# The low part of every fourth weight unit, moved from VectorE to a negating ScalarE pass and an adding DMA

## Chip, core and metric

One core of one Trainium2 chip. The metric is the time of one execution in microseconds on the device; lower is better. The profiler shows the TensorE matmul queue (PE), its weight loads (PEld), VectorE (DVE), ScalarE (ACT), GpSimd (POOL) and the DMA queues of SyncE (SPq) and of GpSimd (POOLq).

## What is computed

Two transformer-like layers follow one another on 256 tokens of width 2048, in float32. Each layer has a mixing part (projections, a state-space or delta-rule scan, an attention) and then the MLP, and only the MLPs are touched here:

```python
u = rmsnorm(x, g_mlp) @ w_up                    # first layer: 2048 -> 8192
x = x + jnp.square(jax.nn.relu(u)) @ w_down     # 8192 -> 2048
...
h = rms_norm(x, ln2_w)                          # second layer
x = x + jnp.square(jax.nn.relu(h @ w_up)) @ w_down
return rms_norm(x, ln_f_w)
```

## The kernel before

**Weights.** Every matmul operand is split in two: a high part in the rounded format `fp32r`, and a low part, the value less its high part. A product is three matmuls: high by high, high by low, low by high (L558 to L560 in the MLPs). Weights come from HBM in pieces of 128 x 2048 floats (1 MB) into `ring`, which has four places; SP issues these transfers in the order of use (L2972), each when the low parts of the piece four places earlier have been made. A piece is two units of 128 x 1024. For unit `u`, ScalarE copies the unit into `w_hi[:, u % 4]` (L2163), which rounds it, and VectorE subtracts that from the ring's value into `w_lo[:, u % 4]` (L1295). ScalarE may start when TensorE is done with unit `u - 4`; TensorE may start unit `u` when `unit_lo` says that its low part is there. There are four places for units, so a unit's place becomes free three units ahead of its first matmul.

**The MLPs.** The first runs over units 122 to 377, the second over units 628 to 883. Each does four rounds `f` of an up part and a down part, both 32 units. A part is four blocks `n` of 512 columns, a block eight units; a unit is 12 matmuls of 512 columns, back to back. Below, the place of a unit in its block is 0 to 7.

**What comes between.** When TensorE has made an up block, ScalarE applies relu and the square (`relu_squared`, L2472 and L2477) ahead of the copy of the next block's place 3; VectorE turns the block in two halves (`turn_up`, L1695), one after its low part of place 4 and one after that of place 5; ScalarE then makes the block's high part (`squared_hi`, L2483) ahead of the copy of place 7; and VectorE makes its low part (L1703). In the first down block of a round, which turns the fourth up block, the first half comes ahead of VectorE's low part of place 3, and `squared_hi` ahead of the copy of place 6. Each engine works through its list in this fixed order, which is written by hand:

```python
for i in range(8):                    # ScalarE, an up block
    if n > 0 and i == 0:
        relu_squared(b - 1)
    split_to(unit + UNITS)            # the copy of unit + 3
    unit += 1
    if n > 0 and i == 3:
        squared_hi(b - 1, hid)
```

**GpSimd.** It does nothing in the MLPs but fold squares for the norms at their ends (L2862) and issue a few transfers there.

Of the kernel before, what the change touches and what calls it, by code (L numbers as in the profile page):

```python
# [165 lines left out]


USE, UNIT_AT = starts(0), starts(1)

LIFTS = {u: n + 1 for n, u in enumerate(USE[name] + i for name in STAGES for i in LIFTED.get(name, ()))}  # L170

# [114 lines left out]
def build(nc, t_in, x_out, bias_rows, x_kept, decays_kept):  # L286
    with ExitStack() as ctx:
# [6 lines left out]
        def sem(name):  # L294
            return ctx.enter_context(nc.semaphore(name))
# [177 lines left out]
        first_loaded = [sem(f"first_half_loaded{i}") for i in range(2)]  # L473
        piece_loaded = [sem(f"piece_loaded{i}") for i in range(PIECES)]
        unit_hi, unit_lo, unit_used = sem("unit_hi_made"), sem("unit_lo_made"), sem("unit_used")
        bank_read = [sem(f"gemm_bank_read{i}") for i in range(3)]
        norm_summed = sem("norm_summed")
        norm_root, norm_rstd = sem("norm_root"), sem("norm_rstd")
# [40 lines left out]
        back_turned, back_added = sem("down_turned_back"), sem("down_added_to_x")  # L519
        tok_squared, tok_gained, ln_loaded = sem("tokens_squared"), sem("tokens_gained"), sem("ln_rows_loaded")  # L520
        gate_folded = sem("gate_squares_folded")
        acum_blocks, decays_saved, decays_loaded = sem("decays_turned"), sem("decays_saved"), sem("decays_loaded")
        tok_summed, tok_root, tok_rstd = sem("tokens_summed"), sem("tokens_root"), sem("tokens_rstd")
        y_dve, y_act = sem("y_scaled_vector"), sem("y_scaled_scalar")

        def bank_done(e, use):

            e.wait_ge(bank_read[use % 3], use // 3 + 1)

        block = ctx.enter_context(nc.Block())  # L530

# [3 lines left out]
        def _(e):  # L535
# [31 lines left out]
            def column(bank, x, first, k_tiles, ready=None):  # L567
                nonlocal unit
                for k in range(0, k_tiles, 2):
                    if k % UNIT_K == 0:  # L570
                        e.wait_ge(unit_lo, unit + 1)
                    if ready and (k == 0 or ready[1][k] != ready[1][k - 1]):
                        e.wait_ge(ready[0], ready[1][k])
                    done = products_of_two(bank, unit, (k % UNIT_K) * P, x, (first + k) * S, k == 0, k == k_tiles - 2)
                    if k % UNIT_K == UNIT_K - 2:
                        done.then_inc(unit_used, 1)
                        unit += 1
                        if k < k_tiles - 2:
                            yield

            def stacked_column(x, ready):
                nonlocal unit, use
                bank = bank_free()
                for k in range(KD):
                    if k % UNIT_K == 0:
                        e.wait_ge(unit_lo, unit + 1)
                    if k % 2 == 0:
                        e.wait_ge(ready[0], ready[1][k])
                    done = e.matmul(bank[:, :], w_hi[:, unit % UNITS, (k % UNIT_K) * P:(k % UNIT_K + 1) * P],
                                    x[:, :, k * S:(k + 1) * S], start=k == 0, stop=k == KD - 1)  # L590
                    if k % UNIT_K == UNIT_K - 1:
                        done.then_inc(unit_used, 1)
                        unit += 1
                use += 1
# [8 lines left out]
            def column_pair(x, ready, in_turn=1, at_four=None):  # L603
                nonlocal unit, use
                banks = []
                for _ in range(2):
                    banks.append(bank_free())
                    use += 1
                for k0 in range(0, KD, in_turn):
                    if k0 == 4 and at_four:  # L610
                        at_four()
                    for j in range(2):
                        for k in range(k0, k0 + in_turn):
                            if j == 0 and k % 2 == 0:
                                e.wait_ge(ready[0], ready[1][k])
                            n = unit + 2 * (k // UNIT_K) + j
                            if k % UNIT_K == 0:
                                e.wait_ge(unit_lo, n + 1)
                            done = products(banks[j], n, (k % UNIT_K) * P, P, x, k * S, k == 0, k == KD - 1)
                            if k % UNIT_K == UNIT_K - 1:  # L620
                                done.then_inc(unit_used, 1)
                unit += 4

            def project_tokens(width, n, x):
                nonlocal unit, use
                banks = []
                for _ in range(2):
                    banks.append(bank_free())
                    use += 1
                per_unit = UNIT // width  # L630
                for k in range(KD):
                    if k % per_unit == 0:
                        e.wait_ge(unit_lo, unit + 1)
# [233 lines left out]
            def up_blocks(m, f, x):  # L867

                nonlocal unit
                for n in range(D // BLOCK):  # L870
                    b = (4 * m + f) * (D // BLOCK) + n
                    for k in range(KD):
# [5 lines left out]
                            if k == 12:  # L878
                                token_norm(2 + 2 * m)
                        if k % 2 == 0:  # L880
                            e.wait_ge(unit_lo, unit + 1)
# [13 lines left out]
            def down_blocks(m, f, hid):  # L895
# [3 lines left out]
                for n in range(D // BLOCK):  # L899
# [5 lines left out]
                    for k in range(KD):  # L905
                        if back and n > 0 and k == 8:
                            turned_back(n - 1)
                        if n == 0 and k % 4 == 0:
                            e.wait_ge(up_lo, b + k // 4 + 1)
                        if k % 2 == 0:  # L910
                            e.wait_ge(unit_lo, unit + 1)
                        for c in range(1 if last and k >= KD // 2 else 2):
                            if k == 0 and n >= 2:
                                e.wait_ge(down_added, 2 * (b - 2) + c + 1)
                            elif k == 0:
                                e.wait_ge(up_read, 2 * (b + 2) + c + 1)
                            done = products_moving(psum[3 + 2 * (n % 2) + c][:, :], unit, (k % 2) * BLOCK, BLOCK, hid,
                                                   k * S + c * P, P, k == 0, k == KD - 1)
                            if c == 0 and k == KD - 1:
                                done.then_inc(down_made, 1)  # L920
                        if k % 2:
                            if not last or k < KD // 2:
                                done.then_inc(unit_used, 1)
                            unit += 1
# [21 lines left out]
            def compress_piece(m, n):  # L946
# [6 lines left out]
                    if m == 1:  # L953
                        e.wait_ge(cmp_act, CMP["act"]["rows"])
                for half in range(2):
                    e.wait_ge(unit_lo, unit + 1)
# [322 lines left out]
        def _(e):  # L1279
            unit = use = made = 0  # L1280

            def split_to(n):

                nonlocal made
                while made < min(n, UNIT_AT["end"]):
                    p, half = unit_of[made]
                    i = made % UNITS
                    e.wait_ge(unit_hi, made + 1)
                    if made // 2 == UNIT_AT["gab"] // 2:
                        hi, w = split(w_hi[:, i, :], UNIT_K), ring[:, p % PIECES, half * UNIT:(half + 1) * UNIT]  # L1290
# [315 lines left out]
            def ssd_output(c):  # L1606
# [2 lines left out]
                yield from rounds(c)  # L1609
                for q4 in range(4):  # L1610
                    g, b, b_act = q4 // 2, len(V) * q4, len(A) * q4
                    e.wait_ge(decays_loaded, 16)
# [537 lines left out]
        def _(e):  # L2150
            unit = use = made = 0

            def split_to(n):

                nonlocal made
                while made < min(n, UNIT_AT["end"]):
# [3 lines left out]
                        e.wait_ge(piece_loaded[p % PIECES], 16 * (p // PIECES + 1))  # L2160
                    if made >= UNITS:
                        e.wait_ge(unit_used, made - UNITS + 1)
                    e.copy(w_hi[:, i, :], ring[:, p % PIECES, half * UNIT:(half + 1) * UNIT]).then_inc(unit_hi, 1)  # L2163
                    made += 1

            def lift(dst):
# [684 lines left out]
        def _(e):  # L2851
# [53 lines left out]
            e.wait_ge(vecs_loaded, 16)  # L2905
            halve_convolutions()
            e.wait_ge(acum_blocks, 1)
            e.dma_start(decays_kept, acum_turned[0:32, :]).then_inc(decays_saved, 16)
            e.wait_ge(decays_saved, 16)
            e.dma_start(mix_plain[:, :, 0:16 * P], decays_spread).then_inc(decays_loaded, 16)  # L2910
# [4 lines left out]
            for g in range(2):  # L2915
# [2 lines left out]
                e.tensor_tensor(sq, sq, ysq[g][1], ALU.add).then_inc(gate_folded, 1)  # L2918
                e.wait_ge(gate_folded, 2 * g + 1)
                e.tensor_tensor(sq[:, 0:S], sq[:, 0:S], sq[:, S:2 * S], ALU.add).then_inc(gate_folded, 1)  # L2920
            gather(1)
            gather(2)
            e.wait_ge(back_added, 8)
            e.dma_start(x_kept, xT).then_inc(x_saved, 16)
# [21 lines left out]
            gather(3)  # L2946
            e.wait_ge(merged_lo, 8)
            e.dma_start(ln_rows, t_in["ln_f_rows"]).then_inc(ln_loaded, 16)

        @block.sync
        def _(e):
# [13 lines left out]
            for n, piece in enumerate(order):  # L2967
                if n < 2:
                    continue
                if n >= PIECES:  # L2970
                    e.wait_ge(unit_lo, split_end[n - PIECES])
                e.dma_start(ring[:, n % PIECES, :], piece).then_inc(piece_loaded[n % PIECES], 16)  # L2972
            for made, count, c, n in ((y_act, 1, 0, 0), (y_dve, 1, 0, 3), (y_act, 2, 0, 1), (y_dve, 2, 0, 2),
                                      (y_act, 3, 1, 0), (y_dve, 3, 1, 3), (y_dve, 4, 1, 2)):
# [125 lines left out]
```

## Time and profile before

| | |
|---|---|
| median of 3 runs | 2630.84 us (2630.72 to 2631.02) |
| span of the profiled execution | 2629.2 us |
| median less this span, for what lies around it | 1.6 us |
| PE busy | 2607.6 us, 99% |
| DVE busy | 1848.5 us, 70% |
| ACT busy | 1309.0 us, 50% |
| POOL busy | 212.9 us, 8% |
| DMA | 483.87 MB, 184 GB/s |

The span runs from the first to the last instruction. Of the profiled execution itself the profile gives only this span and no device time of its own. All times below are in the time of the span.

### The profile page before, as it was taken

The numbers are of one execution on the slowest core, as the hardware profiler recorded it, in microseconds if no ns is written. First come the engines' busy times: TensorE is split into PE (matmuls) and PEld (weight loads), VectorE is DVE, ScalarE is ACT, GpSimd is POOL, SyncE is SP. The second block draws the span as 40 slices with busy tenths as digits, with TensorE's granted clock in tenths as the row PEclk, the third lists the DMA queues.
The fourth block names the chain that finished last, engine by engine and source line by source line (L and its number), as shares of the span: only waits on it lengthen the run. The fifth ranks groups of instructions, "written<-read, shape, count | busy, mean of one in ns | idle before, by whom it ended". The sixth has DMA issues, their size and how long they took to land. (4 is left out here: it accounts for less than half of the span.)

```text
span 2629.2 us, 33722 instructions
## 1 busy us (share of the span) xinstructions
PE 2607.6 (99%) x13388; PEld 2213.5 (84%) x13388; DVE 1848.5 (70%) x2661; ACT 1309.0 (50%) x1823; POOL 212.9 (8%) x188
## 2 busy tenths in 40 slices
PE   9999999999999999999999999999999999999998
PEld 8788888888888888888888888888888888888887
DVE  7788897857658567786776767567658567486685
ACT  6545455435445444565554545455554354454453
POOL 4014011000000000140411300000100000000000
PEclk9999999999999999999999999999999999999999
DMA  7654455555555555576444333355555555555553
GB/s 267 164 212 175 161 176 185 200 192 192 192 192 185 203 188 202 182 260 240 145 145 144 113 129 129 129 211 180 202 193 192 193 191 197 189 190 206 186 201 128
DMA packets 68468, 483.87 MB, mean 184 GB/s; under 512 B 8039, under 2 KB 8183, under 8 KB 11224
## 3 DMA queue, kind: packets, MB, share of 16 engines
q1 hardware_dynamic: 65520, 467.43, 49.6%
q0 software_dynamic: 2272, 12.87, 1.7%
q8 instruction: 106, 1.74, 0.3%
q10 hardware_dynamic: 520, 1.43, 0.1%
q14 instruction: 50, 0.41, 0.0%
HBM read 475.38 MB, written 6.31 MB: 183 GB/s over the span
## 5 line engine op out<-in xcount | busy, mean ns | idle before, releaser
L1295 DVE TENSOR_TENSOR w_lo<-weight_ring,w_hi 128x1024 fp32r<-128x1024 f32 x882 | 1084.6, 1241 | 609.6 <-ACT w_hi L2163 605.7
L2163 ACT CAST w_hi<-weight_ring 128x1024 fp32r<-128x1024 f32 x884 | 916.9, 1048 | 714.9 <-PE bank L560 581.5
L548 PE MATMUL bank<-mix,w_hi 128*128 128x512 f32 x1776 | 567.3, 401 | 3.9 <-DVE arena L1367 1.6
L558 PE MATMUL bank<-w_hi,h 128*128 128x512 f32 x1056 | 412.5, 391 | 0.0
L558 PE MATMUL bank<-w_hi,mix 128*128 128x512 f32 x1056 | 411.2, 389 | 0.0
L560 PE MATMUL bank<-w_hi,h 128*128 128x512 f32 x1056 | 411.0, 389 | 0.0
L559 PE MATMUL bank<-w_lo,h 128*128 128x512 f32 x1056 | 410.9, 389 | 0.0
L559 PE MATMUL bank<-w_lo,mix 128*128 128x512 f32 x1056 | 410.9, 389 | 0.0
L560 PE MATMUL bank<-w_hi,mix 128*128 128x512 f32 x1056 | 410.8, 389 | 0.0
L551 PEld LDWEIGHTS bank<-mix,w_lo 128*128 128x128 f32 x1776 | 333.6, 188 | 78.7
L551 PE MATMUL bank<-mix,w_lo 128*128 128x256 f32 x1776 | 349.7, 278 | 0.0
L548 PE MATMUL bank<-h,w_hi 128*128 128x512 f32 x864 | 280.9, 406 | 0.0
L548 PEld LDWEIGHTS bank<-mix,w_hi 128*128 128x128 f32 x1776 | 271.7, 189 | 7.0 <-DVE arena L1367 2.0
L1695 DVE STREAM_TRANSPOSE arena<-arena 32x256 f32<-32x256 f32 x512 | 223.0, 436 | 23.9 <-ACT arena L2477 16.8
L558 PEld LDWEIGHTS bank<-w_hi,h 128*128 128x128 f32 x1056 | 198.2, 188 | 41.6 <-DVE w_lo L1295 0.7
L560 PEld LDWEIGHTS bank<-w_hi,h 128*128 128x128 f32 x1056 | 198.2, 188 | 41.4
L560 PEld LDWEIGHTS bank<-w_hi,mix 128*128 128x128 f32 x1056 | 198.2, 188 | 41.3
L559 PEld LDWEIGHTS bank<-w_lo,h 128*128 128x128 f32 x1056 | 198.3, 188 | 41.0 <-issue 0.2
L558 PEld LDWEIGHTS bank<-w_hi,mix 128*128 128x128 f32 x1056 | 198.2, 188 | 41.0
L559 PEld LDWEIGHTS bank<-w_lo,mix 128*128 128x128 f32 x1056 | 198.2, 188 | 40.9
L551 PEld LDWEIGHTS bank<-h,w_lo 128*128 128x128 f32 x864 | 162.3, 188 | 38.2
L551 PE MATMUL bank<-h,w_lo 128*128 128x256 f32 x864 | 170.2, 278 | 0.0
(379 smaller groups left out, 1997.7 us busy)
## 6 DMA issues: line engine op xcount, KB each, us to landing
weight_ring<-in_w_up SPq DMA_DIRECT2D x128, 1024.0 KB, 4.7
weight_ring<-in_w_down SPq DMA_DIRECT2D x128, 1024.0 KB, 4.7
weight_ring<-in_w_merge SPq DMA_DIRECT2D x32, 1024.0 KB, 4.8
weight_ring<-in_w_gdn SPq DMA_DIRECT2D x24, 1024.0 KB, 4.8
weight_ring<-in_w_papb SPq DMA_DIRECT2D x16, 1024.0 KB, 4.7
weight_ring<-in_w_o SPq DMA_DIRECT2D x16, 1024.0 KB, 4.7
weight_ring<-in_w_xbc SPq DMA_DIRECT2D x12, 1024.0 KB, 4.7
weight_ring<-in_w_q SPq DMA_DIRECT2D x8, 1024.0 KB, 4.8
```

Source lines behind the costliest of these rows:

```text
L548: e.matmul(bank[:, :], w_hi[:, unit_at % UNITS, o + j * P:o + (j + 1) * P], x[:, :, at + j * S:at + (j + 1) * S], start=first and j == 0, ...
L551: done = e.matmul(bank[:, 0:S], w_lo[:, unit_at % UNITS, o + j * P:o + (j + 1) * P], x[:, 0, at + j * S:at + (j + 1) * S], start=False, st ...
L558: e.matmul(out, x[:, 0, at:at + m], hi, start=first, stop=False)
L559: e.matmul(out, x[:, 0, at:at + m], lo, start=False, stop=False)
L560: return e.matmul(out, x[:, 1, at:at + m], hi, start=False, stop=last)
L1295: e.tensor_tensor(w_lo[:, i, :], ring[:, p % PIECES, half * UNIT:(half + 1) * UNIT], w_hi[:, i, :].bitcast(F32), ALU.subtract).then_inc(un ...
L1695: done = e.transpose(dst[:, :, :, 32 * r:32 * r + 32], src[:, :, :, 32 * q:32 * q + 32])
L2163: e.copy(w_hi[:, i, :], ring[:, p % PIECES, half * UNIT:(half + 1) * UNIT]).then_inc(unit_hi, 1)
```

## The change

Of every four units of the MLPs' weights, the one with `u % 4 == 3` gets its low part in another way: units 123 to 343 of the first MLP (56 of them; the last 32 units of that MLP are left as they were) and 631 to 883 of the second (64). As the first MLP begins at unit 122 and the second at 628, these are places 1 and 5 of a block in the first MLP and places 3 and 7 in the second. ScalarE makes the high part as before and then a second pass, which writes the high part with its sign turned into `w_lo`. Only then does it count up `unit_hi`. GpSimd waits for this count and issues a transfer of 512 KB that adds the unit's float32 weights onto `w_lo`: from the ring in the first MLP, from the weights in HBM in the second. TensorE waits for its landing in place of `unit_lo`; SP, too, waits for landings before it loads over a piece. VectorE leaves these units out. A second pair of semaphores of an earlier transfer is folded into one (`decays_moved`), with the same order of transfers.

```diff
+DMA_LO = [u for u in range(UNIT_AT["mlp"], UNIT_AT["mlp"] + 224) if u % 4 == 3] + [
+    u for u in range(UNIT_AT["mlp2"], UNIT_AT["end"]) if u % 4 == 3]
+DMA_LO_OF = {u: n for n, u in enumerate(DMA_LO)}
...
+        def lo_ready(e, u):
+
+            if u in DMA_LO_OF:
+                e.wait_ge(lo_landed, 16 * (DMA_LO_OF[u] + 1))
+            else:
+                e.wait_ge(unit_lo, vector_los(u + 1))
...
-                        if k % 2 == 0:
-                            e.wait_ge(unit_lo, unit + 1)
+                        if k % 2 == 0:
+                            lo_ready(e, unit)
...
                     i = made % UNITS
+                    if made in DMA_LO_OF:
+                        made += 1
+                        continue
                     e.wait_ge(unit_hi, made + 1)
...
-                    e.copy(w_hi[:, i, :], ring[:, p % PIECES, half * UNIT:(half + 1) * UNIT]).then_inc(unit_hi, 1)
+                    done = e.copy(w_hi[:, i, :], ring[:, p % PIECES, half * UNIT:(half + 1) * UNIT])
+                    if made in DMA_LO_OF:
+                        done = e.activation(w_lo[:, i, :], ring[:, p % PIECES, half * UNIT:(half + 1) * UNIT], ACT.Copy,
+                                            scale=-1.0)
+                    done.then_inc(unit_hi, 1)
...
+            def add_weights(first, end):
+
+                for u in DMA_LO:
+                    if first <= u < end:
+                        p, half = unit_of[u]
+                        w = (ring[:, p % PIECES, half * UNIT:(half + 1) * UNIT] if u < UNIT_AT["mlp2"] else
+                             order[p][:, half * UNIT:(half + 1) * UNIT])
+                        e.wait_ge(unit_hi, u + 1)
+                        e.dma_start(w_lo[:, u % UNITS, :], w, accum_op=ALU.add).then_inc(lo_landed, 16)
+
             gather(1)
+            add_weights(UNIT_AT["mlp"], UNIT_AT["kv"])
             gather(2)
...
+            add_weights(UNIT_AT["mlp2"], UNIT_AT["end"])
...
-                    e.wait_ge(unit_lo, split_end[n - PIECES])
+                    last = split_end[n - PIECES]
+                    e.wait_ge(unit_lo, vector_los(last))
+                    landed = sum(u < last for u in DMA_LO)
+                    if landed:
+                        e.wait_ge(lo_landed, 16 * landed)
```

## Rows read from the trace of the kernel before

**Rows 1.** The page: busy time of two engines, and the two dearest groups.

```profile
PE 2607.6 (99%) x13388; PEld 2213.5 (84%) x13388; DVE 1848.5 (70%) x2661; ACT 1309.0 (50%) x1823; POOL 212.9 (8%) x188
...
L1295 DVE TENSOR_TENSOR w_lo<-weight_ring,w_hi 128x1024 fp32r<-128x1024 f32 x882 | 1084.6, 1241 | 609.6 <-ACT w_hi L2163 605.7
L2163 ACT CAST w_hi<-weight_ring 128x1024 fp32r<-128x1024 f32 x884 | 916.9, 1048 | 714.9 <-PE bank L560 581.5
```

**Rows 2.** Windows inside the two MLPs: length, busy PE, PEld, DVE, ACT, POOL, clock, DMA.

```profile
410.00:1050.00 640.00, 640.00 (x2827) 529.98 (x2826) 429.54 (x537) 296.99 (x319) 2.90 (x2) 1.00 0.54 193
1945.00:2600.00 655.00, 655.00 (x2904) 542.23 (x2903) 437.97 (x545) 305.02 (x334) 0.00 (x0) 1.00 0.54 191
```

**Rows 3.** Waits of PEld, 1925 to 2600 us: total, times, longest; the only row.

```profile
PEld bank L852 <- ACT arena L2487: 0.2, 1, 0.2
```

**Rows 4.** Timeline of a quiet stretch: start, length, what, idle before.

```profile
700.58 0.39 PE L558 MATMUL bank<-w_hi,mix 128*128 128x512 f32 x1
...
700.83 1.05 ACT L2163 CAST w_hi<-weight_ring 128x1024 fp32r<-128x1024 f32 x1 [1.67 <-PE bank L560]
...
701.91 1.23 DVE L1295 TENSOR_TENSOR w_lo<-weight_ring,w_hi 128x1024 fp32r<-128x1024 f32 x1 [1.49 <-ACT w_hi L2163]
...
708.74 0.39 PE L558 MATMUL bank<-w_hi,mix 128*128 128x512 f32 x1
```

**Rows 5.** Timeline, first MLP, an up block: ScalarE, and PE at place 1.

```profile
467.98 2.94 ACT L2163 CAST w_hi<-weight_ring 128x1024 fp32r<-128x1024 f32 x3
...
477.54 0.39 PE L558 MATMUL bank<-w_hi,h 128*128 128x512 f32 x1
```

**Rows 6.** Timeline, second MLP, ScalarE in an up block.

```profile
2121.92 1.14 ACT L2477 ACTIVATE arena<-arena 128x512 f32<-128x512 f32 x2
2122.96 2.20 ACT L2163 CAST w_hi<-weight_ring 128x1024 fp32r<-128x1024 f32 x2
...
2134.81 1.05 ACT L2483 CAST mix<-arena 128x1024 fp32r<-128x1024 f32 x1 [4.21 <-DVE arena L1695]
2135.77 3.00 ACT L2163 CAST w_hi<-weight_ring 128x1024 fp32r<-128x1024 f32 x3
```

**Rows 7.** Timeline of the same block, VectorE.

```profile
2124.03 2.38 DVE L1295 TENSOR_TENSOR w_lo<-weight_ring,w_hi 128x1024 fp32r<-128x1024 f32 x2 [3.06 <-ACT w_hi L2163]
2126.33 3.56 DVE L1695 STREAM_TRANSPOSE arena<-arena 32x256 f32<-32x256 f32 x8
2129.93 1.22 DVE L1295 TENSOR_TENSOR w_lo<-weight_ring,w_hi 128x1024 fp32r<-128x1024 f32 x1
2131.18 3.60 DVE L1695 STREAM_TRANSPOSE arena<-arena 32x256 f32<-32x256 f32 x8
```

**Rows 8.** Timeline, TensorE's first matmuls of places 3 and 7 of that block.

```profile
2129.29 0.39 PE L558 MATMUL bank<-w_hi,h 128*128 128x512 f32 x1
...
2140.17 0.39 PE L558 MATMUL bank<-w_hi,h 128*128 128x512 f32 x1
```

**Rows 9.** Timeline, second MLP, a first down block, VectorE then ScalarE.

```profile
2191.98 2.36 DVE L1295 TENSOR_TENSOR w_lo<-weight_ring,w_hi 128x1024 fp32r<-128x1024 f32 x2
...
2198.95 2.95 ACT L2163 CAST w_hi<-weight_ring 128x1024 fp32r<-128x1024 f32 x3
```

**Rows 10.** DMA issues by line: count, KB each, us from issue to landing.

```profile
weight_ring<-in_w_down SPq DMA_DIRECT2D x128, 1024.0 KB, 4.7
...
x_kept<-arena POOLq DMA_DIRECT2D x1, 2048.0 KB, 7.6
arena<-x_kept POOLq DMA_DIRECT2D x1, 2048.0 KB, 9.9
x_out<-arena SPq DMA_DIRECT2D x7, 256.0 KB, 2.4
...
arena<-in_ln_f_rows POOLq DMA_DIRECT2D x1, 1024.0 KB, 6.7
```

**Rows 11.** Windows over the `x_kept` transfer, issued at 1118.6; columns as in rows 2.

```profile
1118.60:1119.60 1.00, 1.00 (x7) 0.89 (x6) 1.00 (x1) 0.00 (x0) 0.56 (x2) 1.00 0.00 0
1119.60:1126.20 6.60, 6.60 (x38) 5.75 (x38) 5.17 (x7) 3.97 (x6) 0.00 (x0) 1.00 1.00 369
```

**Rows 12.** Waits of SP's queue, 1925 to 2600 us.

```profile
SPq L2972 <- DVE w_lo L1295: 631.2, 123, 7.9
```

More of the change, by code:

```diff
@@ L168, with vector_los @@
 USE, UNIT_AT = starts(0), starts(1)
+DMA_LO = [u for u in range(UNIT_AT["mlp"], UNIT_AT["mlp"] + 224) if u % 4 == 3] + [
+    u for u in range(UNIT_AT["mlp2"], UNIT_AT["end"]) if u % 4 == 3]
+DMA_LO_OF = {u: n for n, u in enumerate(DMA_LO)}
+def vector_los(n):
+    return n - sum(u < n for u in DMA_LO)
 LIFTS = {u: n + 1 for n, u in enumerate(USE[name] + i for name in STAGES for i in LIFTED.get(name, ()))}
@@ L475, in build @@
         unit_hi, unit_lo, unit_used = sem("unit_hi_made"), sem("unit_lo_made"), sem("unit_used")
+        lo_landed = sem("unit_lo_landed")
         bank_read = [sem(f"gemm_bank_read{i}") for i in range(3)]
@@ L521, in build @@
         gate_folded = sem("gate_squares_folded")
-        acum_blocks, decays_saved, decays_loaded = sem("decays_turned"), sem("decays_saved"), sem("decays_loaded")
+        acum_blocks, decays_moved = sem("decays_turned"), sem("decays_moved")
         tok_summed, tok_root, tok_rstd = sem("tokens_summed"), sem("tokens_root"), sem("tokens_rstd")
@@ L585, in stacked_column @@
                     if k % UNIT_K == 0:
-                        e.wait_ge(unit_lo, unit + 1)
+                        lo_ready(e, unit)
                     if k % 2 == 0:
@@ L617, in column_pair @@
                             if k % UNIT_K == 0:
-                                e.wait_ge(unit_lo, n + 1)
+                                lo_ready(e, n)
                             done = products(banks[j], n, (k % UNIT_K) * P, P, x, k * S, k == 0, k == KD - 1)
@@ L632, in project_tokens @@
                     if k % per_unit == 0:
-                        e.wait_ge(unit_lo, unit + 1)
+                        lo_ready(e, unit)
                     for c in range(2):
@@ L880, in up_blocks @@
                         if k % 2 == 0:
-                            e.wait_ge(unit_lo, unit + 1)
+                            lo_ready(e, unit)
                         for c in range(2):
@@ L910, in down_blocks @@
                         if k % 2 == 0:
-                            e.wait_ge(unit_lo, unit + 1)
+                            lo_ready(e, unit)
                         for c in range(1 if last and k >= KD // 2 else 2):
@@ L955, in compress_piece @@
                 for half in range(2):
-                    e.wait_ge(unit_lo, unit + 1)
+                    lo_ready(e, unit)
                     for r in range(per_unit):
@@ L1611, in ssd_output @@
                     g, b, b_act = q4 // 2, len(V) * q4, len(A) * q4
-                    e.wait_ge(decays_loaded, 16)
+                    e.wait_ge(decays_moved, 32)
                     e.tensor_tensor(split(d, 4), split(decay_rows[c][q4], 4),
@@ L2907, in _ @@
             e.wait_ge(acum_blocks, 1)
-            e.dma_start(decays_kept, acum_turned[0:32, :]).then_inc(decays_saved, 16)
-            e.wait_ge(decays_saved, 16)
-            e.dma_start(mix_plain[:, :, 0:16 * P], decays_spread).then_inc(decays_loaded, 16)
+            e.dma_start(decays_kept, acum_turned[0:32, :]).then_inc(decays_moved, 16)
+            e.wait_ge(decays_moved, 16)
+            e.dma_start(mix_plain[:, :, 0:16 * P], decays_spread).then_inc(decays_moved, 16)
             near_taps("xbc", xbcT, "conv_w", XBC_T, conv_accs[0], sq0, 0, "conv_b")
```

## The prediction

> **What bounds the kernel now.** I read the page first. TensorE is busy 99% of the span, VectorE 70%, ScalarE 50%, GpSimd 8%; the two dearest groups off TensorE are the two passes over each weight unit, 1.24 us on VectorE and 1.05 us on ScalarE [rows 1]. A share over the whole kernel says little about a change to the MLPs, so next come windows inside them: TensorE is busy for all of the 640 us and all of the 655 us, at full clock, while VectorE works 430 and 438 us [rows 2]. The reader should see that VectorE has a third of its time free there. Then the view of waits: in the second MLP TensorE waited once, 0.2 us, and not for a low part [rows 3]; in the first, from 409 to 1050 us, that view has no row at all. So relief for VectorE has nothing to give back. What is left to ask is whether the new, longer way to a low part is still short enough, and for that the timeline of a unit is needed.
>
> **The time that a unit has.** In a quiet stretch TensorE starts a unit at 700.58, which frees a place; ScalarE starts its copy at 700.83 and ends at 701.88; VectorE starts its pass at 701.91 and ends at 703.14; TensorE starts on that place at 708.74 [rows 4]. That is 8.16 us for three units, 2.72 each. From the end of the copy to TensorE's start there are 6.86 us, of which VectorE's way uses 1.26.
>
> **What the change removes.** 120 VectorE passes of 1.24 us, 149 us of work on an engine with idle time [rows 1, 2]. What hides it is TensorE's unbroken row of matmuls. Worth nothing on the path, except where VectorE's order delays something else, below.
>
> **What it adds on ScalarE.** 120 passes over the same 128 x 1024 floats. I cost each like the copy, 1.05 us [rows 1], 126 us in all on an engine busy 297 of 640 us [rows 2]: room enough on average, but each pass lies in the new chain of its own unit and ahead of the next copy.
>
> **What it adds on GpSimd and in DMA.** One transfer at a time. Call D the time from its issue to its landing; no row shows an adding transfer, so it must be bounded. Below: SP's 256 KB take 2.4 us and its 1024 KB take 4.7 us [rows 10], so a plain 512 KB takes about 2.4 + 2.3 / 3 = 3.2 us, and I take 3.1 as the low end, since the larger fixed part of GpSimd's queue isn't in these two. An adding transfer, however, must also read what it adds to, so I price it as 1024 KB. On GpSimd's queue the 2048 KB of `x_kept` take 7.6 us, 1.0 of them before any DMA engine moves; the DMA engines are full for the 6.6 that follow [rows 11]. Half of these 6.6 gives 1.0 + 3.3 = 4.3 us. The row of 1024 KB on the same queue says 6.7 us [rows 10]. It came beside loads of the ring. I take **D = 5.0 us**, nearer to the 4.3, because the ring's loads are let go by low parts that are made at other moments than the adding transfer. The high end is the 2048 KB from HBM, 9.9 us [rows 10], should the adding itself run at half the rate.
>
> The Trainium skill, DMA: Bandwidth & Descriptors, section on the anatomy of one DMA on the GpSimd path, gives about 2.0 us plus the bytes over 436 GB/s; as an estimate from that page, 1024 KB would take 4.4 us, and with D = 4.4 the sum below would be +36 us in place of +46. The `x_kept` row, 7.6 us for 2048 KB, is a little over what that rule says (6.8).
>
> **First MLP: the transfer just fits.** The chain from the end of the copy is 1.05 (negating) + 0.1 (GpSimd sees the count; about what the row of VectorE after ScalarE and of ScalarE after TensorE show [rows 4]) + D. It has 6.86 us, so nothing is late while D is below 5.7. The tightest place 1 comes behind three copies in a row, which end at 470.92, against a start of TensorE at 477.54, so 6.62 and D up to 5.5 [rows 5]. With D = 5.0 this MLP costs 0. The cover is then 0.5 to 0.7 us thin.
>
> **Second MLP: places 3 and 7 are the late ones.** Here ScalarE is behind when it comes to exactly these two units.
>
> - Place 3: the copy stands behind relu and square and ends at 2124.0; TensorE starts it at 2129.29 [rows 6, 8]. 5.29 us are there, and 1.05 + 0.1 + D are wanted: late by D - 4.14.
> - Place 7: the copy stands behind `squared_hi`, which waits for VectorE's turned block. It ends at 2135.77 + 1.05 = 2136.82; TensorE starts at 2140.17 [rows 6, 8]. Only 3.35 us are there. And the chain before it gets longer: ScalarE's copy of place 4 now comes after the negating pass of place 3, so it ends 1.05 later, at 2126.1; VectorE's low part of place 4 ends at 2127.35 where it ended at 2126.4; both halves of the turning, `squared_hi` and the copy of place 7 move by 0.95, though VectorE has lost its pass over place 3 [rows 7]. These instructions follow one another with no idle time, so no slack swallows it. Late by D + 0.1 + 1.05 + 0.95 - 3.35 = **D - 1.25**.
>
> Both lie in one block. A stall at place 3 gives VectorE's chain the same time, so the block loses the larger of the two, D - 1.25. The next block's relu waits for TensorE's last matmul, so each block starts with the old distances and loses again: nothing is caught up. An up part turns three blocks within itself, four rounds make 12. The first of the 12 is looser, as its later parts wait for the norm; that leaves 11 that follow the pattern. In the four first down blocks, VectorE's pass over place 3 comes between the halves of the turning [rows 9]; there its removal brings `squared_hi` forward by 1.2, and what decides is place 3, late by about D - 4.1. With the odd up block these are 5.
>
> All other adding transfers, 56 in the first MLP and 32 in the second, have the 5.7 us.
>
> **SP's queue.** The next piece in a place may be loaded when the adding transfer has landed. Before, SP waited 123 times for VectorE in the second MLP, 631 us in all [rows 12]: it is far ahead. In the new kernel a unit lands 0.25 + 2.1 + 0.1 + 5.0 = 7.5 us after its place became free; the load takes 4.7 [rows 10], so 12.2; the same ring place is wanted by ScalarE seven units later, at 19.0. Cover of 6.8 us, so nothing. The merged `decays_moved` counts the same two transfers: nothing. ScalarE's relu, and the copies behind a negating pass, find at least the 1.67 us of idle time of the quiet stretch [rows 4], except in the chain that is already costed.
>
> **Sum.** 11 x (5.0 - 1.25) + 5 x (5.0 - 4.1) = 41.3 + 4.5 = 46 us. On the span of 2629.2 that gives 2675; 1.6 us lie around the span, and the median is 2630.84, so **2677 us**.
>
> **Rivals.**
>
> *The adding is slow.* If D is over 5.7, the 88 transfers with full room are late too, each by D - 5.7. For D = 6.7, as the 1024 KB row, 11 x 5.45 + 5 x 2.6 + 88 x 1.0 = 161 us: 2792. For D = 9.9, 95 + 29 + 370 = 494 us: 3125. For it speaks that no row shows an adding transfer at all, and that 1024 KB on this queue once took 6.7 us; against it, that those 1024 KB shared the DMA engines with the ring. The Trainium skill, Collectives: The Full Stack, section on the bandwidth ceiling, puts the cost of a reducing DMA in its two source reads and not in the addition; no run here has shown it yet.
>
> *The adding is nearly as fast as a plain transfer* (D = 3.1 to 4): 11 x 1.85 = 20 us up to 30 us: 2651 to 2661.
>
> *No slower.* ScalarE and VectorE's chain in the second MLP would have to let go of place 7 earlier, and the landing follow within what is left. If the relief of VectorE brings the turning forward by its 1.2 us in all blocks, as it does in the down blocks, place 7 is late by D - 3.4 - 1.2 + 1.15 = D - 3.45 us, and a plain-like D of 3.2 hides it: 2631. It decides from D below 3.45. Against it stands that VectorE's pass over place 4 waits for ScalarE, not for VectorE. A gain beyond that has no wait to come from [rows 3].
>
> *The clock falls.* Stalls of some 4 us in each block of 21.8 could take the granted clock down; in all of both MLPs it was 1.00 [rows 2], and TensorE never stood still there. If each of 11 blocks ran as long as its stall (3.75 us) at half clock, 2 us of work would be lost 11 times, 21 us more: 2698.
>
> **Chances.** Forecast (D from 4 to 5.7, +30 to +57 us) 0.52; nearly plain 0.10; slow adding 0.28, about half of it above D = 7.4; clock 0.04; no slower 0.06. The low end of the range is the nearly plain case, 2650. The high end is D = 7.4: 11 x 6.15 + 5 x 3.3 + 88 x 1.7 = 234 us, 2865; above it and below 2650 there are 0.2. Within the likeliest case the range is 2661 to 2688. Faster by over 0.2% (about what a measurement of this kernel can tell from none) 0.02, within it 0.05, slower 0.93.
>
> **What would show it.** In the changed kernel's waits, TensorE's rows by the adding transfer into `w_lo`, some 11 of 3.5 to 4 us, all in the second MLP's up parts and at place 7; none in the first. The negating pass at 1.05 us; `squared_hi` 0.95 us later against the block's start. GpSimd's issues with some 5.0 us to landing. TensorE's busy time in the window of the first MLP complete as before. The prediction is wrong if D is over 5.7 (stalls in the first MLP) or under 2, or if the turning isn't delayed.

## The result, and the profile after

The changed kernel takes 2730.6 us (2725.9 to 2734.0, 4 runs) against 2630.9: slower, ratio 1.0377 (1.0363 to 1.0392), 99.7 us. The forecast was 2677, range 2650 to 2865. Sign and range hold; the size is twice the forecast. The profiled execution has a span of 2732.2 us against 2629.2.

Windows over the two MLPs and what lies between, first of the kernel before (length, busy PE, PEld, DVE, ACT, POOL, clock, DMA share, GB/s):

```profile
409.00:1108.60 699.60, 699.60 (x3103) 579.54 (x3102) 469.66 (x580) 326.02 (x357) 8.44 (x7) 1.00 0.54 192
1108.60:1920.90 812.30, 808.57 (x4989) 714.71 (x4988) 575.19 (x940) 431.79 (x731) 117.77 (x104) 1.00 0.47 170
1920.90:2621.80 700.90, 700.87 (x3110) 579.91 (x3108) 460.76 (x571) 326.05 (x362) 3.42 (x3) 1.00 0.53 188
```

and of the changed one:

```profile
408.90:1121.80 712.90, 703.43 (x3103) 580.74 (x3102) 403.92 (x526) 379.34 (x412) 56.33 (x63) 1.00 0.73 230
1121.80:1933.60 811.80, 808.50 (x4989) 714.80 (x4988) 575.10 (x940) 431.58 (x731) 118.81 (x104) 1.00 0.48 170
1933.60:2724.80 791.20, 733.91 (x3110) 590.89 (x3108) 385.73 (x507) 385.92 (x426) 57.66 (x67) 0.97 0.69 209
```

The first MLP grew by 13.3 us, the second by 90.3, and what lies between by nothing. VectorE lost 66 and 75 us of work, ScalarE gained 53 and 60, somewhat less than the 56 and 64 passes at 1.24 and 1.05 us (69 and 79, 59 and 67). In the second MLP TensorE's busy time grew too, by 33 us with the same count of matmuls, and the granted clock is 0.97: that is no wait, and the prediction had put it into a rival.

The changed kernel's page, the answers to [rows 1] (busy; costliest groups with mean, idle before them and its releaser) and its DMA issues:

```profile
PE 2644.3 (97%) x13388; PEld 2225.9 (81%) x13388; DVE 1706.1 (62%) x2541; ACT 1422.8 (52%) x1943; POOL 316.2 (12%) x308
...
L1316 DVE TENSOR_TENSOR w_lo<-weight_ring,w_hi 128x1024 fp32r<-128x1024 f32 x762 | 939.8, 1242 | 822.2 <-ACT w_hi L2184 819.2
...
L576 PE MATMUL bank<-w_hi,h 128*128 128x512 f32 x1056 | 424.9, 402 | 52.1 <-DMA w_lo<-in_w_up 44.5
L576 PE MATMUL bank<-w_hi,mix 128*128 128x512 f32 x1056 | 414.7, 393 | 14.5 <-DMA w_lo<-in_w_down 12.4
...
w_lo<-weight_ring POOLq DMA_DIRECT2D x56, 512.0 KB, 4.5
w_lo<-in_w_up POOLq DMA_DIRECT2D x32, 512.0 KB, 5.4
```

The adding transfer, D in the prediction, takes 4.5 us from the ring and 5.4 us from HBM (medians), on either side of the 5.0 taken. The groups of TensorE that had no idle time before now have 52 and 14 us, nearly all released by the adding transfers of the second MLP. The first MLP's waits for such transfers are one row more (total, times, longest), and 7.0 us of it are a single wait at its start:

```profile
PE bank L576 <- DMA w_lo<-weight_ring: 9.3, 5, 7.0
```

**A block with both places.** The second MLP, round 1, block 2; ScalarE, GpSimd and TensorE:

```profile
2184.44 1.31 ACT L2497 ACTIVATE arena<-bank,arena 128x512 f32<-128x512 f32 x2 [3.63 <-PE bank L578]
...
2187.62 1.05 ACT L2186 ACTIVATE w_lo<-weight_ring 128x1024 fp32r<-128x1024 f32 x1
...
2199.28 1.05 ACT L2508 CAST mix<-arena 128x1024 fp32r<-128x1024 f32 x1 [4.96 <-DVE arena L1716]
2200.23 1.05 ACT L2184 CAST w_hi<-weight_ring 128x1024 fp32r<-128x1024 f32 x1
2201.18 1.05 ACT L2186 ACTIVATE w_lo<-weight_ring 128x1024 fp32r<-128x1024 f32 x1
```

```profile
2188.97 0.86 POOL L2954 DMA_DIRECT2D w_lo<-in_w_up  x1 [11.58 <-ACT w_lo L2186]
2202.53 0.86 POOL L2954 DMA_DIRECT2D w_lo<-in_w_up  x1 [12.70 <-ACT w_lo L2186]
```

```profile
2190.30 0.39 PE L576 MATMUL bank<-w_hi,h 128*128 128x512 f32 x1
2194.44 0.50 PE L576 MATMUL bank<-w_hi,h 128*128 128x512 f32 x1 [1.26 <-DMA w_lo<-in_w_up]
...
2197.30 0.39 PE L576 MATMUL bank<-w_hi,h 128*128 128x512 f32 x1
...
2202.74 0.39 PE L576 MATMUL bank<-w_hi,h 128*128 128x512 f32 x1
...
2207.82 0.50 PE L576 MATMUL bank<-w_hi,h 128*128 128x512 f32 x1 [2.20 <-DMA w_lo<-in_w_up]
2208.15 0.52 PE L577 MATMUL bank<-w_lo,h 128*128 128x512 f32 x1
2208.47 0.63 PE L578 MATMUL bank<-w_hi,h 128*128 128x512 f32 x1
2208.90 0.63 PE L576 MATMUL bank<-w_hi,h 128*128 128x512 f32 x1
...
2212.25 0.40 PE L576 MATMUL bank<-w_hi,h 128*128 128x512 f32 x1
```

Each of these starts but those of 2208 is the first matmul of a unit: places 2, 3, 4, 6, 7 and the next block's 0. A unit takes 2.72 us. From place 2 to 3 it is 4.14 (1.42 lost), from 6 to 7 it is 5.08 (2.36 lost): 3.8 in the block, where D - 1.25 gives 4.15 with D = 5.4. The pass ends at 2202.23, GpSimd issues 0.3 us later, not 0.1. Two things come on top. After the shorter wait the unit takes 2.86 us in place of 2.72. And after the longer wait the matmuls start 0.43 us apart instead of 0.23: TensorE's clock has fallen, and this unit takes 4.43 us. The window over that stretch has the clock in its last but two column:

```profile
2208.30:2211.70 3.40, 3.40 (x10) 2.62 (x9) 0.00 (x0) 0.00 (x0) 0.00 (x0) 0.50 0.77 282
```

Half is the lower of the clock's two levels, 1.2 GHz in place of 2.4. The unit is 1.57 us longer than the one after the shorter wait, so a drop costs some 1.6 us.

**The starts.** ScalarE's pass over unit 123, GpSimd's queue and TensorE as the first MLP begins, then GpSimd's queue at the second:

```profile
404.56 1.05 ACT L2186 ACTIVATE w_lo<-weight_ring 128x1024 fp32r<-128x1024 f32 x1
```

```profile
411.25 1.28 POOL L2887 TENSOR_TENSOR arena<-arena 128x512 f32<-128x512 f32 x1 [3.35 <-ACT arena L2256]
412.61 1.59 POOL L2889 TENSOR_TENSOR arena<-arena 128x256 f32<-128x256 f32 x1
414.14 0.92 POOL L2954 DMA_DIRECT2D w_lo<-weight_ring  x1
```

```profile
418.83 0.77 PE L576 MATMUL bank<-w_hi,h 128*128 128x512 f32 x1 [6.99 <-DMA w_lo<-weight_ring]
```

```profile
1937.91 0.58 POOL L2984 DMA_DIRECT2D arena<-in_ln_f_rows  x1
1938.49 0.91 POOL L2954 DMA_DIRECT2D w_lo<-in_w_up  x1
```

ScalarE had negated unit 123 by 405.6, but GpSimd works through its list in order, and `gather(1)`, the folding of the norm's squares, stands first. The transfer leaves 8.5 us late, TensorE waits 7.0 us, and the clock falls. The same folding stands in the kernel before, 2.90 us of GpSimd's time in the window of the first MLP [rows 2]: it reaches into the MLP's start, and not only its end. In the second MLP the first transfer comes right behind a load of 1 MB on the same queue and takes 8.0 us to land; TensorE waits 4.6 us.

### The profile page after: what moved, and what is told of

Read it like the earlier page. It is cut to its first block and busy times, and to the rows that moved or that the text cites. A ratio compares the mean times of both kernels' runs of the same rounds, so it can differ in the third digit from the quotient of the medians.

```text
span 2732.2 us, 34219 instructions
## 1 busy us (share of the span) xinstructions
PE 2644.3 (97%) x13388; PEld 2225.9 (81%) x13388; DVE 1706.1 (62%) x2541; ACT 1422.8 (52%) x1943; POOL 316.2 (12%) x308
## 5 line engine op out<-in xcount | busy, mean ns | idle before, releaser
L1316 DVE TENSOR_TENSOR w_lo<-weight_ring,w_hi 128x1024 fp32r<-128x1024 f32 x762 | 939.8, 1242 | 822.2 <-ACT w_hi L2184 819.2
L576 PE MATMUL bank<-w_hi,h 128*128 128x512 f32 x1056 | 424.9, 402 | 52.1 <-DMA w_lo<-in_w_up 44.5
L577 PE MATMUL bank<-w_lo,h 128*128 128x512 f32 x1056 | 419.3, 397 | 0.0
L578 PE MATMUL bank<-w_hi,h 128*128 128x512 f32 x1056 | 419.0, 397 | 0.0
L576 PEld LDWEIGHTS bank<-w_hi,h 128*128 128x128 f32 x1056 | 203.4, 193 | 106.9 <-DMA w_lo<-in_w_up 50.3
L578 PEld LDWEIGHTS bank<-w_hi,h 128*128 128x128 f32 x1056 | 203.0, 192 | 43.8
```

Source lines behind the costliest of these rows:

```text
L576: e.matmul(out, x[:, 0, at:at + m], hi, start=first, stop=False)
L577: e.matmul(out, x[:, 0, at:at + m], lo, start=False, stop=False)
L578: return e.matmul(out, x[:, 1, at:at + m], hi, start=False, stop=last)
L1316: e.tensor_tensor(w_lo[:, i, :], ring[:, p % PIECES, half * UNIT:(half + 1) * UNIT], w_hi[:, i, :].bitcast(F32), ALU.subtract).then_inc(un ...
```

## The experiments

All edits are to the changed kernel, and times are medians beside before on the same chip (2630.7 to 2631.4).

**1. Roomy places in the second MLP (e1_places15).**

```diff
-    u for u in range(UNIT_AT["mlp2"], UNIT_AT["end"]) if u % 4 == 3]
+    u for u in range(UNIT_AT["mlp2"], UNIT_AT["end"]) if u % 4 == 1]
```

> The second MLP's adding transfers are moved from places 3 and 7 of a block to places 1 and 5, the same number (64) and the same bytes. Theory (place): the loss comes from where in ScalarE's and VectorE's order the unit stands. At places 1 and 5 there are 6.86 us from the end of the copy to TensorE's start, and negating 1.05, 0.3 to GpSimd's issue and 5.4 to the landing need 6.75, so the second MLP loses only some 2 us at its first transfer, about 1 us at its end and a few tenths in the transfers that come later than the median; the first MLP keeps its 13. Total 2645 to 2655. TensorE's clock stays at its full level in the second MLP but for its start. Rival (traffic): the transfers cost wherever they stand, through the DMA engines or the clock: over 2690.

2683.2 us, ratio 1.0197 (1.0182 to 1.0212). Between the two: 47 us of the 100 are gone with the place alone, and the mean clock is 0.994 where it was 0.990, but it is 28 us over the top of what the theory gave. Its waits and landings show why:

```profile
PE bank L576 <- DMA w_lo<-in_w_up: 14.1, 4, 10.7
PE bank L576 <- DMA w_lo<-in_w_down: 13.7, 10, 2.3
```

```profile
DMA to landing us min/median/max: 5.3/5.5/8.0
```

One wait alone is 10.7 us: unit 629 is wanted two units earlier than 631, while GpSimd is still folding squares, and its transfer then takes 7.8 us behind the same 1 MB load. The other 17 us are transfers with a median of 5.5 us and a tail to 8.0 in a room that ends at some 5.5. So place is a cause and start another; a room of just the median is too small.

**2. The first MLP alone (e2_first_only).**

```diff
-DMA_LO = [u for u in range(UNIT_AT["mlp"], UNIT_AT["mlp"] + 224) if u % 4 == 3] + [
-    u for u in range(UNIT_AT["mlp2"], UNIT_AT["end"]) if u % 4 == 3]
+DMA_LO = [u for u in range(UNIT_AT["mlp"], UNIT_AT["mlp"] + 224) if u % 4 == 3]
```

> Only the first MLP's 56 transfers are kept. Both theories take the two MLPs as independent: before plus the 13.3 us that the first MLP grew by in the trace, 2644, within 3 us. Under a rival in which something of the first MLP is paid back or paid again later (the projections between the MLPs, GpSimd's queue), it is off that by more.

2644.2 us, 1.0049 (1.0033 to 1.0066), +13.1. That is what the window of the first MLP had grown by (13.3), so the MLPs are independent; the second is the place to look.

**3. Copying instead of adding (e3_plain).** The low parts are then whole weights, so the output is another one.

```diff
-                        e.dma_start(w_lo[:, u % UNITS, :], w, accum_op=ALU.add).then_inc(lo_landed, 16)
+                        e.dma_start(w_lo[:, u % UNITS, :], w).then_inc(lo_landed, 16)
```

> The transfers only copy, without adding: same 512 KB, same queue, same sources; the low parts are then the whole weights, so the output is not the reference's. Theory of the prediction (the adding is priced by its second read): a plain 512 KB takes 3.2 to 3.5 us from issue to landing against 4.5 (ring) and 5.4 (HBM), so place 7 is late by about 2.1 in each of 11 blocks and place 3 by nothing: second MLP +25 to +30 us, total 2665 to 2675. Rival (the cost is GpSimd's issue and descriptors, or HBM's latency, and not the adding): the same 4.5 and 5.4 us to landing and about 2730.

2672.8 us, 1.0157 (1.0142 to 1.0172). The landings, by source:

```profile
w_lo<-weight_ring POOLq DMA_DIRECT2D x56, 512.0 KB, 2.9
w_lo<-in_w_up POOLq DMA_DIRECT2D x32, 512.0 KB, 3.5
```

Adding costs 1.6 to 1.9 us of the 4.5 and 5.4. The prediction's two prices can be held against this: a plain transfer at 3.1 to 3.2 us lies between 2.9 and 3.5, and an adding one priced as 1024 KB, 4.3 us, is near the 4.5 from the ring and 1.1 us short of the 5.4 from HBM. That the extra time is the second read, and not the addition, is not shown by this run, which takes away both. In time, adding is 58 of the 100 us; a plain transfer would still have been 42 us too slow.

**4. ScalarE's pass without the transfer (e4_negate_only).**

```diff
-DMA_LO = [u for u in range(UNIT_AT["mlp"], UNIT_AT["mlp"] + 224) if u % 4 == 3] + [
+NEGATED = [u for u in range(UNIT_AT["mlp"], UNIT_AT["mlp"] + 224) if u % 4 == 3] + [
...
+DMA_LO = []
...
-                    if made in DMA_LO_OF:
+                    if made in NEGATED:
```

> ScalarE makes the negated pass for the same 120 units, but no transfer is issued: VectorE makes every low part again, over the negated one. Theory (it is the transfer's length that is paid, the ScalarE pass is only a part of the chain): at place 7 of the second MLP 3.35 us less 2.0 for the two passes less 1.26 for VectorE leave 0.1 us, so 2631 to 2634. Rival (ScalarE's extra pass itself delays the turning and all that follows): over 2640.

2632.5 us, 1.0005 (0.9996 to 1.0015). 120 more passes on ScalarE, 111 us of busy time (1309.0 to 1420.2), cost nothing that can be told from none.

**5. Each place alone (e6_place7, e7_place3),** in the second MLP only, with `DMA_LO` as

```diff
+DMA_LO = [u for u in range(UNIT_AT["mlp2"], UNIT_AT["end"]) if (u - UNIT_AT["mlp2"]) % 8 == 7]
```

and `== 3`.

> Only place 7 of the second MLP (32 transfers), none in the first. Without the pass ahead of place 4 the copy of place 7 comes as in the kernel before, so place 7 is late by 5.4 + 0.3 + 1.05 - 3.35 = 3.4 in 11 blocks (37 us), by 2.2 in the four first down blocks (9), by 0.9 in the odd one, about 4 at the last block, 0.15 at each restart (2), and 3 to 8 for the clock: 2685 to 2692. The rival reading (place 7 costs its 2.5 us as seen in the trace of after, and place 3 the rest): 11 x 2.5, so about 2670.

2700.1 us, 1.0265 (1.0248 to 1.0281).

> Only place 3 of the second MLP (32 transfers). Late by 5.4 + 0.3 + 1.05 - 5.29 = 1.45 in 15 blocks (22 us), 0.15 at each restart (2), 5 at the first transfer of the MLP, 0 to 5 for the clock: 2660 to 2666. If the two places add up, this and the run with place 7 alone give more in sum than the second MLP's 90 us; if a stall at place 3 gives time to the chain of place 7, as the prediction has it, a block with both loses 3.95 and not 1.45 + 3.4.

2662.8 us, 1.0121 (1.0104 to 1.0138). The waits of the first, then of the second:

```profile
PE bank L575 <- DMA w_lo<-in_w_up: 35.1, 12, 3.3
PE bank L575 <- DMA w_lo<-in_w_down: 12.8, 6, 3.6
```

```profile
PE bank L575 <- DMA w_lo<-in_w_up: 17.4, 12, 4.3
PE bank L575 <- DMA w_lo<-in_w_down: 5.7, 5, 1.3
```

Place 7 alone waits 3 us a block, though the block with both waited only 2.2 there: the 1.3 at place 3 had been given to its chain, as the prediction has it. With both, a block waits 3.5 us (1.26 and 2.20 in the one above), less than the sum of 3.1 and 1.2 for each alone. Place 7 came out 8 us over my upper figure, which had 3 to 8 us for the clock; the mean clock is 0.990 to 0.993 over its four runs, against 0.997 for place 3 alone, where a block's waits are 1.0 to 1.4 us. In sum the two lose 68.7 and 31.4, 100 us, against 87 (99.7 less 13.1) together.

**6. The ring as source in the second MLP too (e8_from_ring).**

```diff
-                        w = (ring[:, p % PIECES, half * UNIT:(half + 1) * UNIT] if u < UNIT_AT["mlp2"] else
-                             order[p][:, half * UNIT:(half + 1) * UNIT])
+                        w = ring[:, p % PIECES, half * UNIT:(half + 1) * UNIT]
```

> The changed kernel with the second MLP's transfers reading the ring as in the first, not HBM. Theory: D falls from 5.4 to 4.5 us there, so 11 blocks lose 0.9 less each (10 us), the five others too (4 us), and the first transfer and the clock some 5 us less: 2706 to 2714. Rival (the source is of no account, the median differs for another reason): 2730.

2709.9 us, 1.0301 (1.0286 to 1.0316), with a median of 4.5 us to landing over all 120. So the source is what makes 4.5 and 5.4, and 0.9 us of it is worth 21 us.

**7. Without the first transfers and the last (e9_no_ends).** `DMA_LO` begins at unit 127 and 635 and ends at 879.

```diff
+DMA_LO = [u for u in range(UNIT_AT["mlp"] + 5, UNIT_AT["mlp"] + 224) if u % 4 == 3] + [
+    u for u in range(UNIT_AT["mlp2"] + 7, UNIT_AT["end"] - 4) if u % 4 == 3]
```

> The changed kernel, but the first transfer of each MLP and the last of the second are left to VectorE (117 stay). Theory: at the starts and the end stands a cost of its own, which the prediction left out. In the trace of after it is 7.5 us of stall and 1.7 of clock at unit 123 (GpSimd is still folding the norm's squares when the unit is ready), 5.1 and some 3 at unit 631 (8.0 us to landing), 3.9 and about 1 for unit 883, whose block is run at half a unit's length: 22 us, so 2704 to 2713. Rival: the next transfer inherits it, 2725 or more.

2709.3 us, 1.0295 (1.0279 to 1.0310). Three transfers of 120 cost 21 us.

**8. The negated pass behind the next copy (e10_negate_later),** for place 3 of the up blocks 1 to 3 of the second MLP:

```diff
                     done.then_inc(unit_hi, 1)
+                    if made - 1 in PUT_OFF:
+                        pn, hn_ = unit_of[made - 1]
+                        e.activation(w_lo[:, (made - 1) % UNITS, :], ring[:, pn % PIECES, hn_ * UNIT:(hn_ + 1) * UNIT],
+                                     ACT.Copy, scale=-1.0).then_inc(unit_hi, 1)
```

> In the up blocks 1 to 3 of each round of the second MLP, ScalarE makes the negated pass of place 3 behind the copy of place 4, no longer ahead of it. Theory: the pass ahead of place 4 holds back VectorE's turning and so place 7 by 0.95 us, and a block loses the later of its two landings, counted from its start. Place 3 then loses some 2.5 alone and place 7 another 0.5, 3.0 in the block instead of 3.95: 11 x 0.95 = 10 us less, 2716 to 2723. Rival (the two places' stalls add up, whatever the order): place 3 loses a microsecond more and place 7 a microsecond less, 2728 to 2735.

2713.5 us, 1.0317 (1.0300 to 1.0334). ScalarE's relu and `squared_hi` of one block:

```profile
2175.90 1.31 ACT L2507 ACTIVATE arena<-bank,arena 128x512 f32<-128x512 f32 x2 [1.54 <-PE bank L584]
...
2190.00 1.05 ACT L2518 CAST mix<-arena 128x1024 fp32r<-128x1024 f32 x1 [4.22 <-DVE arena L1722]
```

14.10 us lie between them. In the changed kernel it was 14.84 (2184.44 to 2199.28 above). The pass ahead of place 4 therefore held the turning back by 0.74, where 0.95 was forecast. In this run place 3 waits 2.1 to 2.4 us in these blocks and place 7 at most 0.7, so a block loses the later of its two landings and not their sum, and the rival (2728 or more) is out. The gain of 17 us is above the 10 that this term was to give. Eleven times 0.74 is 8 us, and in the trace of this run the clock falls three times in rounds 1 to 3 where the changed kernel's does eight times; at 1.6 us each that is 8 more.

**9. The high products first (e11_high_first).** In a unit with an adding transfer:

```diff
+                e.wait_ge(unit_hi, u + 1)
...
+                            e.matmul(bank[c], x[:, j, k * S + c * P:k * S + (c + 1) * P], hi, start=False, stop=False)
+                lo_ready(e, u)
...
+                        done = e.matmul(bank[c], x[:, 0, k * S + c * P:k * S + (c + 1) * P], lo, start=False,
+                                        stop=k == KD - 1)
```

> In a unit with an adding transfer TensorE does the eight products with the high part first and waits for the landing only ahead of the four with the low part, which gives each transfer 8 x 0.227 = 1.8 us more room (not in the first two blocks of each MLP, nor in the last). Theory: 11 blocks lose 2.15 instead of 3.95 (20 us), four others nothing instead of 1.45 (6), the long transfers of the other places some 7, restarts 2, and the clock no longer falls, as it did not in the run with plain transfers, whose stalls were 2.1 (12): 2675 to 2692. Rival (the stalls are not the landings' lateness, so room doesn't help): over 2710.

2685.7 us, 1.0208 (1.0193 to 1.0223). 1.8 us of room are worth 45 us, in the range of the theory, and the rival, over 2710, is out: the stalls are landings that come late.

**10. Waits filled with matmuls (e12_filled_waits).**

```diff
+                        if m and f > 0 and n > 0 and k == KD - 2:
+                            e.wait_ge(unit_hi, unit + 1)
+                            for _ in range(10):
+                                e.matmul(psum[0][:, :], x[:, 0, 0:P], w_hi[:, unit % UNITS, 0:BLOCK], start=True, stop=True)
                         if k % 2 == 0:
                             lo_ready(e, unit)
```

> In the up blocks 1 to 3 of rounds 1 to 3 of the second MLP, TensorE makes ten more matmuls into an unused bank ahead of its wait at place 7: 2.3 us of work within a stall of 2.5; their results are not used. Theory: eight of the drops of the granted clock (3.4 us at half, 1.6 us each) come from TensorE standing still in these waits; filled, they are gone and nothing else changes: 13 us less, 2715 to 2722. Rival (the clock has another cause, or the drops cost nothing): 2728 to 2735.

2716.4 us, 1.0325 (1.0309 to 1.0340). The window over rounds 1 to 3, changed kernel, then this one:

```profile
2060.00:2690.00 630.00, 590.39 (x2506) 476.03 (x2505) 306.85 (x392) 306.79 (x330) 45.62 (x53) 0.98 0.72 218
```

```profile
2060.00:2680.00 620.00, 602.60 (x2626) 490.49 (x2625) 311.26 (x397) 309.71 (x332) 45.16 (x53) 1.00 0.73 223
```

(The windows are of different length and don't hold the same units, so their counts differ by more than the 90.) More work on TensorE, 90 matmuls, makes the kernel 14 us faster, for the clock is back at 1.00 there. Shown: the drops come from TensorE standing still, and the eight of them in these rounds cost 14 us.

**11. All the room (e5_roomy, e13_roomy_high_first).** Places 1 and 5 in both MLPs, from the ring, without the ends; then the high products first as well.

```diff
+DMA_LO = [u for u in range(UNIT_AT["mlp"] + 5, UNIT_AT["mlp"] + 224) if u % 4 == 3] + [
+    u for u in range(UNIT_AT["mlp2"] + 5, UNIT_AT["end"] - 8) if u % 4 == 1]
```

> Places 1 and 5 in both MLPs, the second MLP adds from the ring too, and the first transfer of each MLP and those of the second MLP's last block are left to VectorE (115 transfers stay). Theory (every loss is a landing later than its own room of 5.5 us or so): what is left are the transfers that take over 5.5 us, some 3 to 4 us in each MLP; 2636 to 2642. Rival (the adding traffic or the longer ScalarE work costs in itself): over 2655. Neither theory has it below before, as TensorE has nothing to gain.

2645.9 us, 1.0058 (1.0043 to 1.0073): 14.6 us over before, 4 more than my upper figure. (116 transfers stay, not the 115 of the expectation.)

> Both edits that gave room: places 1 and 5 in both MLPs from the ring without the ends, and the products with the high part first. A transfer then has some 7.3 us (5.5 in the first two blocks of each MLP). Theory: the 14.6 us that the roomy version still loses are transfers that take 5.5 to 8.0 us to land and the drops of the clock behind them; with 1.8 us more room only those over 7.3 us are left, some three of 0.5 us: 2632 to 2636. Rival (part of the 14.6 us is traffic or longer ScalarE work that no room takes away): 2639 or more.

2634.1 us, 1.0012 (1.0003 to 1.0021), 3.4 us over before. With 116 adding transfers still there, TensorE's waits for them have shrunk to this:

```profile
PE bank L576 <- DMA w_lo<-weight_ring: 1.6, 1, 1.6
PE bank L898 <- DMA w_lo<-weight_ring: 1.2, 2, 0.9
```

```profile
DMA to landing us min/median/max: 4.5/4.7/8.4
```

What is left of the waits are a few transfers of up to 8.4 us. The DMA traffic and the ScalarE passes together cost no more than these 3.4 us; and even so there is no gain, since VectorE's relief had nothing to give.

## Why the prediction was right in sign and half in size

Right, by its steps:

- *What bounds it.* TensorE never waited for a low part, so relief of VectorE was worth nothing. The best of all forms, with VectorE relieved of 116 passes, is still 3.4 us above before.
- *ScalarE's pass at 1.05 us, in itself free:* 1.06 measured, and +1.4 us for all 120, with an interval that includes none (experiment 4).
- *The first MLP just fits* in the typical block. Its +13.1 us are the start with its fall of the clock and a few long transfers: the four waits behind the first add up to 2.3 us.
- *Places 3 and 7, and no catching up.* The place is worth 47 us (experiment 1), a block with both loses one chain and not two (experiments 5 and 8), and the pass ahead of place 4 delays the turning (experiment 8), by 0.74 us rather than 0.95.
- *D = 5.0:* 4.5 and 5.4, the higher where it was needed. With D = 5.4 the prediction's own sum gives 52 us (11 x 4.15 + 5 x 1.3) in place of 46. By the rule of the Trainium skill, DMA: Bandwidth & Descriptors, section on the anatomy of one DMA on the GpSimd path, 1024 KB would take 4.4 us, an estimate; the trace agrees for the ring (4.5) and is 1.0 us above it for HBM (5.4). The Trainium skill, Collectives: The Full Stack, section on the bandwidth ceiling, puts the cost of a reducing DMA in its second read; experiment 3 has adding at 1.6 and 1.9 us, and no run here tells the read from the addition.

That 2730.6 lies in the range is luck: the likeliest case ended at 2688, and what the range had above that, the clock rival at 2698 aside, stood there for an adding transfer of more than 5.7 us, which its medians of 4.5 and 5.4 are not.

The step that failed is the **Sum**. Its pattern, 11 and 5 blocks, measured some 48 us (11 x 3.8, 4 x 1.4, and 0.5 in the odd up block) against 46 forecast. That a block's 3.8 is so near the 3.75 is in part luck: D (5.3 there) and GpSimd's issue came out 0.3 and 0.2 us longer, the delay of the turning and the pass behind its copy (0.95 from end to end) 0.2 and 0.1 us shorter. The rest of the 100 is in four terms that it did not have:

- *"All other adding transfers have the 5.7 us."* Three don't: the first of the first MLP, behind `gather` in GpSimd's queue, the first of the second, behind a load of 1 MB there, and unit 883, whose block is run with half a unit's matmuls per step and so is wanted earlier. 21 us (experiment 9). The work queued ahead of the new instructions on GpSimd was in front of me in the diff, and I didn't count it.
- *The clock.* Priced as a rival of 0.04 and 21 us. It happened: eight drops in rounds 1 to 3, 14 us (experiment 10), two more in round 0, some 3 us, and those behind the two starts and unit 883, which are in the 21.
- *The tail of D.* The first MLP's landings reach 6.5 us with a median of 4.5, the second's 6.9 with 5.4 (and 8.0 the first of all), and a room of some 5.5 holds only the median. In the trace ten waits outside the pattern and the ends add up to 6.2 us, some 8 us with the late starts behind them, an estimate. In experiment 11 room removes 11 of 14.6.
- *Restarts:* 0.13 to 0.18 us in the unit after each of the 37 waits that are not those three, 5 us. GpSimd's issue, 0.3 us behind ScalarE and not 0.1, is in the 3.8 already.

48 + 21 + 17 + 8 + 5 is 99, against 99.7 in the medians and 103 in the span of the trace. The 21 and 14 of the 17 are differences of runs, the others are read from one trace, so a few microseconds could stand under another term.

What stays open is why single transfers take 6 to 8 us. They come in every run with adding transfers, with either source, and experiment 3's plain ones show them too (5.9 us at the longest). But they are not spread at random. In the changed kernel's trace, SP's queue and GpSimd's at a transfer that took 6.5 us (the first of the two loads in the row starts at 688.04), and its landing:

```profile
688.04 8.04 SPq L3013 DMA_DIRECT2D weight_ring<-in_w_down  x2
```

```profile
689.22 0.86 POOL L2954 DMA_DIRECT2D w_lo<-weight_ring  x1 [10.02 <-ACT w_lo L2186]
```

```profile
DMA to landing us min/median/max: 6.5/6.5/6.5
```

Over the traces of all runs with adding transfers, 40 of these were issued 1.0 to 1.9 us behind a load of the ring, all 40 at place 5 of a round's first down block. Each took 5.5 us or more, at least 1.0 us over the median of its MLP. The load just ahead and the place come together, so these traces cannot tell which it is; other long ones have no such load just ahead, and no run moved a load to test it.

## What to carry to other kernels

When a hand-over is made longer, its cost is lateness against a room, and the room differs by place: read it at every kind of place in the cycle, at the first and last instance, and against the slowest landings, not the median. For an engine that gets new work, list what already stands in its queue. A bound engine that is made to wait can pay twice, once for the wait and once in clock, as TensorE did here; if a wait can't be avoided, put work that is ready ahead of it.

## What was not expected of the hardware

- An adding transfer of 512 KB on GpSimd's queue takes 4.5 us from SBUF and 5.4 us from HBM, a plain one 2.9 and 3.5.
- With waits of 2.1 to 2.5 us TensorE's clock fell from 2.4 to 1.2 GHz for 3.4 us, in eight of the nine up blocks 1 to 3 of rounds 1 to 3. With waits of 1.0 to 1.4 us (place 3 alone) the mean clock was 0.997, and its one fall inside an MLP came with the first wait, of 4.3 us.
- Ninety needless matmuls in those waits made the kernel 14 us faster.
- The 40 adding transfers that were issued less than 2 us behind a 1 MB load of the ring all took 5.5 to 8.4 us, against medians of 4.5 to 5.5.
